# The four block sums of the down projection's activations, moved from VectorE to GpSimd

## The reference, cut to what matters

```python
h = _rmsnorm(x, g_fp)
f = (jax.nn.silu(h @ w_g) * (h @ w_u)) @ w_d      # w_d: (2816, 1024)
x = x + _rmsnorm(f, g_fq)
```

## Time and profile before

| | us |
|---|---|
| time, median of 3 runs (lowest to highest) | 1453.59 (1453.14 to 1455.04) |
| the profiled execution's own time | 1453.83 |
| its span in the profile | 1452.1 |
| TensorE busy | 1434.0 (99%) |
| VectorE busy | 875.2 (60%) |
| ScalarE busy | 627.8 (43%) |
| GpSimd busy | 322.2 (22%) |

### The profile page before, as it was taken

The page is one execution under the profiler, slowest core; times in us unless marked ns, Lnnn a source line. Parts: engine busy times, 40 slices in busy tenths (PEclk is TensorE's granted clock), DMA queues, the critical chain, the costliest instruction groups (busy, mean ns, idle before and its releaser), DMA issues.

```text
span 1452.1 us, 26576 instructions
## 1 busy us (share of the span) xinstructions
PE 1434.0 (99%) x10633; PEld 1387.8 (96%) x10633; DVE 875.2 (60%) x1539; ACT 627.8 (43%) x1259; POOL 322.2 (22%) x288
## 2 busy tenths in 40 slices
PE   7999999999999999999999999999999999999998
PEld 6999999999999999997789999999999999999997
DVE  7735766313424438483678966777775667667565
ACT  7335555335524532244676433333333335443561
POOL 2022222000000016060002354655362220010111
PEclk9999999999999999999999999999999999999999
DMA  7112323613212126215564334555543349223632
GB/s 233 30 50 77 97 79 112 184 57 108 73 30 77 30 87 205 61 54 176 196 200 140 99 120 153 193 179 204 167 146 118 95 148 377 82 81 108 228 141 102
DMA packets 168381, 184.90 MB, mean 127 GB/s; under 512 B 17514, under 2 KB 128370, under 8 KB 166852
## 3 DMA queue, kind: packets, MB, share of 16 engines
q1 hardware_dynamic: 164368, 171.09, 36.6%
q0 software_dynamic: 2720, 7.89, 1.8%
q10 hardware_dynamic: 1172, 4.23, 0.7%
HBM read 140.73 MB, written 42.45 MB: 126 GB/s over the span
## 4 chain that ended last, share of the span: by engine, by line
PE 93%; DVE 4%; DMA 1%; ACT 1%; issue 1%; DVEq 0%; ACTq 0%
PE bank L1057 7%; PE bank L1059 6%; PE bank L1058 6%; PE psAB L1601 3%; PE bank L1601 3%; PE psAB L1603 3%; PE psAB L1602 3%; PE bank L1602 3%; PE bank L1603 3%; PE psT L1053 3%; PE bankC L1603 2%; PE bankC L1601 2%; PE bankC L1602 2%; PE bank L1158 2%; PE bank L1160 2%; PE bank L1159 2%
## 5 line engine op out<-in xcount | busy, mean ns | idle before, releaser
L1057 PE MATMUL bank<-h_hi,w_hi 128*128 128x344 f32 x464 | 155.8, 336 | 3.0 <-DVE h_lo L2472 3.0
L1059 PE MATMUL bank<-h_hi,w_lo 128*128 128x344 f32 x464 | 149.3, 322 | 0.0
L1058 PE MATMUL bank<-h_lo,w_hi 128*128 128x344 f32 x464 | 149.2, 322 | 0.0
L2229 ACT ACTIVATE s_hi<-raw 128x512 fp32r<-128x512 f32 x126 | 78.7, 627 | 106.7 <-PE psAB L1603 91.3
L1601 PE MATMUL psAB<-f,s_hi 128*128 128x258 f32 x400 | 113.5, 284 | 0.1
L1603 PE MATMUL psAB<-f,s_lo 128*128 128x258 f32 x400 | 112.7, 282 | 0.0
L2459 DVE TENSOR_TENSOR w_lo<-w_raw,w_hi 128x1024 fp32r<-128x1024 f32 x53 | 65.5, 1235 | 61.3 <-ACT w_hi L1764 61.3
L3027 DVE TENSOR_TENSOR s_lo<-raw,s_hi 128x512 fp32r<-128x512 f32 x126 | 94.7, 778 | 2.7 <-ACT s_hi L2229 2.6
L1057 PEld LDWEIGHTS bank<-h_hi,w_hi 128*128 128x128 f32 x464 | 88.3, 190 | 7.3 <-POOL w_lo L3329 3.2
L1601 PE MATMUL bank<-f,s_hi 128*128 128x258 f32 x328 | 93.0, 283 | 0.6 <-DVE ev L3207 0.4
L1603 PE MATMUL bank<-f,s_lo 128*128 128x258 f32 x328 | 92.6, 282 | 0.0
(11 more groups left out here) (686 smaller groups left out, 4937.0 us busy)
## 6 DMA issues: line engine op xcount, KB each, us to landing
raw<-in_w_gate SPq DMA_DIRECT2D x26, 512.0 KB, 4.9
raw<-in_w_up SPq DMA_DIRECT2D x26, 512.0 KB, 6.2
w_raw<-in_w_in SPq DMA_DIRECT2D x24, 512.0 KB, 4.4
w_raw<-in_w_out SPq DMA_DIRECT2D x24, 512.0 KB, 3.7
tp<-in_w_down SPq DMA_DIRECT2D x22, 512.0 KB, 4.6
t_rows<-tp SPq DMA_DIRECT2D x11, 1024.0 KB, 5.1
a_rows<-ab SPq DMA_DIRECT2D x18, 516.0 KB, 2.7
sx_raw<-in_w_in SPq DMA_DIRECT2D x18, 512.0 KB, 5.1
```

Source lines behind the costliest of these rows:

```text
L1057: mm(out[:, 0:TG], w_hi[par][:, ws], hi[:, k, tgc[tg]], start=first, stop=False)
L1058: mm(out[:, 0:TG], w_hi[par][:, ws], lo[:, k, tgc[tg]], start=False, stop=False)
L1059: return mm(out[:, 0:TG], w_lo[par][:, ws], hi[:, k, tgc[tg]], start=False, stop=last)
L2229: fn(slot(q, 0), split_source(q), ACT.Copy).then_inc(sp_hi, 1)
```

## The change

The function `a_sum` is taken out of VectorE's program and put into GpSimd's. VectorE's table `SUM_AT`, which placed the twelve pieces between its low parts, is gone. GpSimd makes the pieces of S3 and then S2 back to back behind its last weight sums, then the three squares of product 1, then S1 and S4 back to back, then the squares of product 4. The order within each sum, its pieces and its operands are the same. Two waits are new, since VectorE's own order no longer gives them: S1 waits for `al_s` of 11 (A11's low parts are made) and S4 for 22 (A12's).

```diff
-            def a_sum(name, p):
...
-            SUM_AT = {(0, 9): ("S3", 1), (0, 11): ("S3", 2), (0, 13): ("S3", 0), (1, 5): ("S2", 0), (1, 8): ("S2", 1),
...
-                    if (x, k) in SUM_AT:
-                        a_sum(*SUM_AT[x, k])
...
+            def a_sum(name, p):
+
+                k, kn = A_PIECES[p]
+                b11, b12, b21, b22 = (b[:, k:k + kn, :] for b in a_blk)
+                if name == "S3":
+                    pool.wait_ge(a_in[p], A_BEFORE[p] + 32)
+                    ins = g_.tensor_tensor(b21, b11, b21, ALU.subtract)
+                elif name == "S2":
+                    if p:
+                        pool.wait_ge(a_in[3 + p], A_BEFORE[3 + p] + 32)
+                    else:
+                        pool.wait_ge(a1_in, 16)
+                    pool.wait_ge(sa_s, 8 + 3)
+                    ins = g_.tensor_tensor(b22, b22, b21, ALU.subtract)
+                elif name == "S1":
+                    pool.wait_ge(sa_s, 8 + 6)
+                    pool.wait_ge(al_s, KH)
+                    ins = g_.tensor_tensor(b11, b22, b11, ALU.add)
+                else:
+                    pool.wait_ge(al_s, 2 * KH)
+                    ins = g_.tensor_tensor(b12, b12, b22, ALU.subtract)
+                ins.then_inc(sa_s, 1)
...
+            pool.wait_ge(sa_s, 8)
+            for p in (1, 2, 0):
+                a_sum("S3", p)
+            for p in range(3):
+                a_sum("S2", p)
             for m in (1, 2, 3):
                 add_square(1, m)
+            for p in range(3):
+                a_sum("S1", p)
+            for p in range(3):
+                a_sum("S4", p)
             for m in (1, 2, 3):
                 add_square(4, m)
```

More of the change, by code:

```diff
@@ L3278, in _ @@
                 job(j)
-            SUM_AT = {(0, 9): ("S3", 1), (0, 11): ("S3", 2), (0, 13): ("S3", 0), (1, 5): ("S2", 0), (1, 8): ("S2", 1),
-                      (1, 10): ("S2", 2), (2, 5): ("S1", 0), (2, 8): ("S1", 1), (2, 10): ("S1", 2), (3, 5): ("S4", 0),
-                      (3, 8): ("S4", 1), (3, 10): ("S4", 2)}
             for x in range(6):
```

## The result

The changed kernel takes 1486.81 us (median of 4 runs, 1486.04 to 1488.28) against 1453.37 for the kernel before in the same sessions: a ratio of 1.0232 (95% interval 1.022 to 1.0244), 33.4 us slower. The forecast was 1487.5 us, with a range of 1472 to 1498. The profiled execution took 1486.33 us, its span is 1484.6.

What follows compares the result with a forecast made beforehand. TensorE was taken to bound the kernel, busy 1434.0 of 1452.1 us. Delays of 17.8 and 16.2 us, clock included, sum to 34.0 on the profiled 1453.83, giving 1487.8; against the median, 1487.5 us, range 1472 to 1498.

Steps and rivals of the forecast that it cites:

- A piece's price: GpSimd's sums: 5.8 us for 2580 numbers, 3.55 for 1548; with a low part between, periods of 6.2 and 4.0 us.
- One low part a hand-over: Where GpSimd has pieces queued, VectorE gets one low part a piece and waits out each whole piece; chance 0.78.
- The first run: S3 and S2, six pieces: TensorE waits for low(8) and low(9), and is 15.2 us late at step 10 without the clock.
- The second run: S1 and S4, six pieces: TensorE's steps 26, 27 and 28 late by 2.3, 9.6 and 14.7 us without the clock.
- The clock: After TensorE's long waits, half clock for 6.1 us costs 3.05; the runs become 17.8 and 16.2 us, 4.5 for the clock.
- Two low parts a hand-over: Rival, both runs: each period 0.6 us longer but brings two low parts; sum 20.3, 1477 us with the clock; chance 0.12.
- a hold that ends early: Rival, every low part of both runs: waits about half a microsecond, TensorE doesn't wait; 1453.6 us, no change; chance 0.08.
- a gain from VectorE's relief: Rival: less VectorE work ahead of the tail makes the kernel faster, 1453.3 us at best; chance of faster 0.02.

Runs made afterwards that it cites:

- write-only kernel: The changed kernel with each of the twelve pieces as a GpSimd memset of the same block, the sums left out: 1452.90 us, ratio 0.9994.
- kernel without sums: The changed kernel with the S sums left out, each piece a GpSimd memset of one number a partition: 1453.86 us, ratio 1.0002.
- the cut by two: The changed kernel with every GpSimd piece cut into instructions of at most two tiles (1032 numbers), 28 in place of 12: 1477.96 us, ratio 1.0167.
- the copy: The changed kernel with each piece as a GpSimd copy of one block (one SBUF input), the sums left out: 1454.88 us, one run.
- one tile with S4 later: The changed kernel with every piece cut into instructions of one tile (516 numbers) and S4 kept until low(38) is made: 1453.28 us, ratio 1.0004.
- the runs of three: The changed kernel with its two runs of six whole pieces broken into four of three, S2 waiting for low(16), S4 for low(38): 1460.04 us, ratio 1.0054.

## Why the prediction was right

- **A piece's price.** Predicted 6.2 and 4.0 us a period; measured S3's three in 14.05 us and S2's in 13.62, against 14.2. Right, and the cheaper end (2.07 ns a number) was as near.
- **One low part a hand-over, held for the whole instruction.** This was carried from 516 numbers to 2580 with no row in between, and held. The Trainium skill's page "SBUF — State Buffer", section "Who interferes with whom", has the rule; by it a memset must not hold, which the write-only kernel shows too.
- **The first run.** Predicted 15.2 us without the clock, measured 14.8. But the pieces of it were not in the place that I gave them: a_low(8) began at 1219.44, just ahead of GpSimd's first piece at 1219.57, where I had it wait for that piece. Everything after stood one low part further on: low(8) ended at 1234.2 and not 1241.0, low(9) at 1244.1 and not 1249.0. A21's landing, 7.2 us after issue for 6.8, decided it. TensorE's waits were so 1.7, 8.9 and 2.8 us at steps 8, 9 and 10, where I had 7.5 at step 8. The end of the run sets low(10) all the same, 1248.5 for 1250.2, so this error of the path did not reach the total.
- **The second run.** Predicted 14.7 us, measured 14.3: steps 26, 27 and 28 late by 2.3, 9.4 and 14.3 for 2.3, 9.6 and 14.7.
- **The clock.** Predicted 2.6 + 1.5 in the stage. Measured 1.6 + 1.5: it was back 3.4 us after the last wait of the run and not 6.1 as in the earlier trace rows. Those 6.1 us were one profile's: in the changed kernel's own start the granted clock is 0.70 from 18 to 21 us and 1.00 from 21 on. The tail's 1.6 us I had not predicted. In the profiled executions the tail made up for what the first clock term and the holds fell short, and the 1.1 us from ahead of the stage came off: 32.5. That 34.0 is as near to this, and to the 33.4 between the medians, as it is, is luck; the 29.1 us of the holds against 29.9 are not.
- **The rivals.** Two low parts a hand-over, a hold that ends early, and a gain from VectorE's relief are refuted by the rows above, the last by the kernel without sums.
- **Open.** Why the granted clock falls in the tail in some profiles (the changed kernel, the cut by two, the copy, one tile with S4 later) and not in the other eight wasn't tested. TensorE had no wait over 0.1 us in the tail ahead of these drops, and none near 588 us in the kernel before. Five of the nine profiles in which pieces hold VectorE off have no drop in the tail either, and the other three (before, write only, no sums) have none; that is too few to say that holds play no part.

## What to carry to other kernels

Before work is moved from VectorE to GpSimd, look whether both read SBUF at that time: here VectorE's instructions with two SBUF inputs waited out every GpSimd sum and copy that read there, up to 6.2 us, and got in once for each of them. What it costs is not GpSimd's time but VectorE's lead in that stretch, so either cut the work so that the period is shorter than the consumer's need (not run here: the shortest period was 1.7 us, where TensorE wants a low part every 1.44), or space the pieces by a wait on the work that they would starve; and look at what stands behind the held instructions in their queue. And if the engine that is relieved isn't waited for, as here, there is nothing to gain, however busy it is.

## What the runs showed of the hardware that I had not expected

A GpSimd memset of 1548 numbers (1.40 us) left VectorE's low parts at 0.68 us, where a copy of 2580 (2.68 us, one SBUF input) made one 2.82 us long. And a wait of TensorE of 2.1 us, at step 26 of the runs of three, was already followed by a granted clock of 0.50 for 3.4 us, while one of 1.7 us, at step 8 of the same kernel, was not, nor one of 2.6 us at step 10 of the kernel cut by two (1.00 from 1236 to 1244 us). So the length of the wait alone does not decide it. It falls without a wait too: for 3.4 us near 588 us in five of the twelve profiles, which is worth 1.5 us there and moves all that comes behind. Who compares start times of two profiles far into a kernel has to look for such stretches first.
